# The last layer norm of a one-layer decoder step: statistics of two token tiles and the sample rows on ScalarE, the sample rows' normalising on ScalarE and GpSimd

## What is computed

```python
def layer_norm(x, g, b):
    xf = x.astype(F32)
    mu = jnp.mean(xf, -1, keepdims=True)
    var = jnp.mean(jnp.square(xf - mu), -1, keepdims=True)
    return ((xf - mu) * lax.rsqrt(var + LN_EPS) * g.astype(F32) + b.astype(F32)).astype(x.dtype)
...
xp = layer_norm(DN_ALPHA * xp + ff, ln2_g[l], ln2_b[l])
y_prompt = xp[:, N_META:]
...
xs = layer_norm(DN_ALPHA * xs + ff, ln2_g[l], ln2_b[l])
```

## Time and profile before

| | |
|---|---|
| time, median of three executions | 1506.05 us (1503.6, 1506.05, 1509.25) |
| span of the profiled execution, first to last instruction | 1499.4 us |
| TensorE busy | 1348.8 us, 90% |
| VectorE busy | 437.9 us, 29% |
| ScalarE busy | 327.1 us, 22% |
| GpSimd busy | 316.9 us, 21% |
| mean granted TensorE clock | 0.957 |
| VectorE's work in the last norm | 1474.05 to 1496.60 us |

### The profile page before, as it was taken

How to read it: one execution, slowest core, us unless ns; L and a number is a source line. 1 busy time by engine, 2 the same in 40 slices (tenths; PEclk the granted TensorE clock), 3 DMA queues, 4 the chain that set the end, 5 groups by cost and what they waited for, 6 DMA issues and landing times.

```text
span 1499.4 us, 32889 instructions
## 1 busy us (share of the span) xinstructions
PE 1348.8 (90%) x13060; PEld 663.9 (44%) x13060; DVE 437.9 (29%) x1016; ACT 327.1 (22%) x760; POOL 316.9 (21%) x328
## 2 busy tenths in 40 slices
PE   7999899889799999898999989899998988999980
PEld 6878677655423343232434323343433333333330
DVE  2311553757643221111221112122111311211225
ACT  1103001550003132122223212231321213222120
POOL 5214200112512122211112211111221111131012
PEclk9999998799779999999999999999999999999995
DMA  9355011350368999999999999999999999999953
GB/s 304 74 122 94 14 38 35 96 229 29 141 259 339 410 406 406 409 412 411 408 411 404 405 410 412 408 405 409 400 408 413 409 408 400 408 401 410 417 204 118
DMA packets 100515, 460.85 MB, mean 307 GB/s; under 512 B 30482, under 2 KB 40862, under 8 KB 51200
## 3 DMA queue, kind: packets, MB, share of 16 engines
q1 hardware_dynamic: 81440, 426.48, 70.5%
q0 software_dynamic: 18336, 30.14, 8.1%
q10 hardware_dynamic: 592, 2.13, 0.4%
HBM read 442.21 MB, written 22.37 MB: 310 GB/s over the span
## 4 chain that ended last, share of the span: by engine, by line
PE 42%; DMA 21%; DVE 8%; SPq 6%; issue 2%; ACT 0%; ACTq 0%; POOL 0%; DVEq 0%; POOLq 0%
PE PS L1379 19%; DMA ring<-in_w_moe_dram 19%; PE PS L1401 14%; PE PS L1281 4%; SPq L489 4%; DVE mix L1954 2%; PE PS L1392 1%; PE PS L1361 1%; DVE qmT L1961 1%; DVE qmT L1959 1%; SPq L497 1%; PE PS L1371 1%; DVE qmT L1955 1%; DVE qmT L1958 1%; DMA smalls<-token_lists 1%
## 5 line engine op out<-in xcount | busy, mean ns | idle before, releaser
L1379 PE MATMUL PS<-ring,mix 128*32 128x512 f32 x5376 | 605.8, 598 | 52.9 <-DMA ring<-in_w_moe_dram 41.9
L1379 PEld LDWEIGHTS PS<-ring,mix 128*32 128x32 f32 x5376 | 165.0, 110 | 453.4 <-issue 346.2
L769 POOL DMA_INDIRECT expert_rows<-mix,smalls x84 | 112.4, 1339 | 796.0 <-issue 510.6
L1954 DVE TENSOR_TENSOR mix<-PS,kn 128x512 f32<-128x512 f32 x84 | 58.1, 692 | 575.0 <-PE PS L1379 569.6
L965 ACT ACTIVATE mix<-PS,smalls 32x256 f32<-32x256 f32 x336 | 156.9, 467 | 177.4 <-PE PS L1401 174.3
L1401 PE MATMUL PS<-ring,mix 128*32 128x256 f32 x3328 | 187.0, 380 | 0.0
L1401 PEld LDWEIGHTS PS<-ring,mix 128*32 128x32 f32 x3328 | 104.7, 110 | 69.5 <-issue 0.5
L949 ACT COPY mix<-PS 128x512 f32<-128x512 f32 (+1 forms) x48 | 24.0, 535 | 466.3 <-PE PS L1371 466.3
L760 POOL DMA_INDIRECT mix<-x_rows,smalls x84 | 87.0, 1035 | 59.7 <-issue 53.1
L1051 PE MATMUL PS<-xT,ring 128*128 128x280 f32 x384 | 96.0, 412 | 0.0
L1039 PE MATMUL PS<-ring,xT 128*128 128x256 f32 (+1 forms) x480 | 86.9, 370 | 0.6 <-ACT mix L826 0.4
(11 more groups left out here) (376 smaller groups left out, 974.7 us busy)
## 6 DMA issues: line engine op xcount, KB each, us to landing
ring<-in_w_moe_dram SPq DMA_DIRECT2D x320, 1024.0 KB, 21.4
xT<-in_w_moe_dram SPq DMA_DIRECT2D x32, 1024.0 KB, 23.7
X<-in_w_moe_dram SPq DMA_DIRECT2D x32, 1024.0 KB, 27.0
ring<-in_w_in_dram SPq DMA_DIRECT2D x9, 1024.0 KB, 17.6
ring<-in_w_out_dram SPq DMA_DIRECT2D x4, 1024.0 KB, 5.0
X<-in_x_prompt_dram SPq DMA_DIRECT2D x4, 512.0 KB, 5.5
ring<-in_state_mlstm_C_dram POOLq DMA_DIRECT2D x1, 2048.0 KB, 16.2
ring<-in_w_in_dram SPq DMA_DIRECT2D x8, 256.0 KB, 10.5
```

What stands on the lines that cost most here:

```text
L769: nc.gpsimd.indirect_dma_start(out=y_dram, out_offset=bass.IndirectOffsetOnAxis(ap=lists[a][0:32, g, 1:2].bitcast(U32), axis=0), in_=ysb[g ...
L1379: ins = mm(bank(BANK0[a] + g)[32 * t:32 * t + 32, :], xgT[XBUF[a][g]][:, P * (k % 2) + 32 * (k // 2):P * (k % 2) + 32 * (k // 2) + 32], sl ...
L1954: link(V.tensor_tensor(ht, bank(BANK0[a] + g), b1b, ALU.add))
```

## The change

- SyncE loads the sample rows third instead of fifth, and stores them last, after the wait for `z_small` instead of the fifth `f_done`.
- VectorE makes `bn_stats` statistics of tiles 0 and 1 alone, both ahead of the first wide pass. It makes all eight wide passes of the prompt tiles; for tiles 2 and 3 they take negative mean and rstd from `zneg` and `zsq`, which come from the other engines. It does nothing for the sample rows.
- ScalarE sums the rows of the sample rows, tile 2 and tile 3 (`row_sums`, an Identity activation with an accumulated output, written to unused PSUM), and after GpSimd has made the negative mean it sums the squares of z - mean (`row_squares`). It also makes (z - mean) * rstd of the sample rows.
- GpSimd makes the means (`mean_of`), the powers of all five tiles (`counted_spread`, `spread_of`), the product -mean * rstd of the sample rows (`zbias`), and multiplies the sample rows by the gain and adds the bias, 8 x 1024 elements each. These are one fixed sequence.
- 16 columns of `smalls` and six semaphores are new. No other part of the program is edited.

```diff
--- before.py
+++ after.py
@@ -255,13 +255,13 @@
         cst = ctx.enter_context(nc.sbuf_tensor("cst", [P, 4, P], F32))
         ident, strict, causal, ones = (cst[:, i, :] for i in range(4))
         GC = ctx.enter_context(nc.sbuf_tensor("GC", [P, NT + 1, 68], F32))
-        sm_t = sb("smalls", 1280)
+        sm_t = sb("smalls", 1300)
         small_at = [0]
 
         def sml(n, rows=P):
             a = small_at[0]
             small_at[0] += n
-            assert small_at[0] <= 1280
+            assert small_at[0] <= 1300
             return sm_t[0:rows, a:a + n]
 
         def chunk(s):
@@ -389,6 +389,8 @@
         gsum = sml(5)
         tokid = sml(5)
         cadd, prime = sml(2), sml(4 * PRIME, 1)
+        zsum, zsq, zneg = sml(NT + 1), sml(NT + 1), sml(NT + 1)
+        zbias = sml(1, NS)
         lists = [sml(2 * n).bitcast(I32).rearrange("p (g c) -> p g c", c=2) for n in (4, 2, 4, 2)]
         raw = [sml(4 * n).rearrange("p (g w) -> p g w", w=4) for n in (4, 2, 4, 2)]
         def by_half(v, half):
@@ -440,6 +442,7 @@
         y_out = [sem(f"y_out{i}") for i in range(4)]
         gt_mm, gt_cp, b2_mm, y_ready = (sem(n) for n in ("gt_mm", "gt_cp", "b2_mm", "y_ready"))
         f_done, y_set, f_chain = (sem(n) for n in ("f_done", "y_set", "f_chain"))
+        z_sum, z_mean, z_sq, z_pow, z_unit, z_small = (sem(n) for n in ("z_sum", "z_mean", "z_sq", "z_pow", "z_unit", "z_small"))
         s_abc, s_scaled, gt_ready = sem("s_abc"), sem("s_scaled"), sem("gt_ready")
         steps = sem("steps")
         x_in = [sem(f"x_in{i}") for i in range(NT + 1)]
@@ -614,15 +617,14 @@
             for b in range(4, 6):
                 sp.wait_ge(xg_in[b], 16 * ROUNDS * XUSE[b])
             sp.wait_ge(shift_out, 32)
-            for tt in range(NT + 1):
+            for tt in (0, 1, NT, 2, 3):
                 r = NS if small(tt) else P
                 sp.dma_start(zb[tt][0:r, :], y_dram[P * tt:P * tt + r, :]).then_inc(x_in[tt], 16)
-            for tt in range(NT + 1):
+            for tt in range(NT):
                 sp.wait_ge(f_done, tt + 1)
-                if small(tt):
-                    sp.dma_start(y_sample.rearrange("b o d -> (b o) d"), zb[tt][0:NS, :]).then_inc(fin_out, 16)
-                else:
-                    sp.dma_start(y_prompt[0, P * tt:P * tt + P, :], zb[tt]).then_inc(fin_out, 16)
+                sp.dma_start(y_prompt[0, P * tt:P * tt + P, :], zb[tt]).then_inc(fin_out, 16)
+            sp.wait_ge(z_small, 1)
+            sp.dma_start(y_sample.rearrange("b o d -> (b o) d"), zb[NT][0:NS, :]).then_inc(fin_out, 16)
             sp.wait_ge(fin_out, 16 * (NT + 1))
 
 
@@ -794,14 +796,39 @@
                     for g in range(GROUPS[2]):
                         scatter(q * 4 + PER * ROUNDS, 2, g, [q * 16 + 16 * (ROUNDS * YUSE[b] + PRIME) for b in range(4)])
 
-            for tt in range(NT + 1):
+            def mean_of(n, tt):
                 r = NS if small(tt) else P
+                pool.wait_ge(z_sum, n + 1)
+                nc.gpsimd.tensor_scalar(zneg[0:r, tt:tt + 1], zsum[0:r, tt:tt + 1], -1.0 / D, None, ALU.mult).then_inc(z_mean, 1)
+
+            def spread_of(n, tt):
+                r = NS if small(tt) else P
+                o = zsq[0:r, tt:tt + 1]
+                pool.wait_ge(z_sq, n + 1)
+                link(nc.gpsimd.tensor_scalar(o, o, 1.0 / D, EPS, ALU.mult, ALU.add))
+                link(nc.gpsimd.tensor_tensor(o, o, powc[0:r, 0:1], ALU.pow), z_pow)
+                if small(tt):
+                    nc.gpsimd.tensor_tensor(zbias, zneg[0:r, tt:tt + 1], o, ALU.mult).then_inc(z_pow, 1)
+
+            def counted_spread(tt):
                 pool.wait_ge(ln_stat, NT + tt + 2)
-                if tt >= 2:
-                    pool.wait_ge(f_done, tt - 1)
-                o = rs2[0:r, tt % 2, 0:1]
-                link(nc.gpsimd.tensor_scalar(o, bag[0:r, 2 * (tt % 2) + 1:2 * (tt % 2) + 2], 1.0, EPS, ALU.mult, ALU.add))
-                nc.gpsimd.tensor_tensor(o, o, powc[0:r, 0:1], ALU.pow).then_inc(ln_pow, 1)
+                o = rs2[:, tt, 0:1]
+                link(nc.gpsimd.tensor_scalar(o, bag[:, 2 * tt + 1:2 * tt + 2], 1.0, EPS, ALU.mult, ALU.add))
+                nc.gpsimd.tensor_tensor(o, o, powc[:, 0:1], ALU.pow).then_inc(ln_pow, 1)
+
+            zs = zb[NT][0:NS, :]
+            mean_of(0, NT)
+            counted_spread(0)
+            mean_of(1, 2)
+            counted_spread(1)
+            spread_of(0, NT)
+            mean_of(2, 3)
+            spread_of(1, 2)
+            pool.wait_ge(ln_in, 64)
+            pool.wait_ge(z_unit, 1)
+            link(nc.gpsimd.tensor_tensor(zs, zs, lng[0:NS, :], ALU.mult))
+            spread_of(2, 3)
+            nc.gpsimd.tensor_tensor(zs, zs, lnb[0:NS, :], ALU.add).then_inc(z_small, 1)
 
 
         @block.scalar
@@ -1003,6 +1030,28 @@
                         if g:
                             weighted(group, 2, g - 1, q * 16 + 16 * (ROUNDS * YUSE[g - 1] + PRIME))
                     weighted(group, 2, 3, q * 16 + 16 * (ROUNDS * YUSE[3] + PRIME))
+
+            aside = PS[:, 0:2, :].rearrange("p b n -> p (b n)")
+
+            def row_sums(tt):
+                r = NS if small(tt) else P
+                act.wait_ge(x_in[tt], 48 if small(tt) else 32)
+                link(nc.scalar.activation(aside[0:r], zb[tt][0:r, :], ACT.Identity, accum_out=zsum[0:r, tt:tt + 1]), z_sum)
+
+            def row_squares(n, tt):
+                r = NS if small(tt) else P
+                act.wait_ge(z_mean, n + 1)
+                link(nc.scalar.activation(aside[0:r], zb[tt][0:r, :], ACT.Square, bias=zneg[0:r, tt:tt + 1],
+                                          accum_out=zsq[0:r, tt:tt + 1]), z_sq)
+
+            row_sums(NT)
+            row_sums(2)
+            row_squares(0, NT)
+            row_sums(3)
+            row_squares(1, 2)
+            act.wait_ge(z_pow, 2)
+            nc.scalar.activation(zb[NT][0:NS, :], zb[NT][0:NS, :], ACT.Identity, scale=zsq[0:NS, NT:NT + 1], bias=zbias).then_inc(z_unit, 1)
+            row_squares(2, 3)
 
 
         @block.tensor
@@ -1997,24 +2046,25 @@
             dve.wait_ge(ln_in, 64)
 
             def row_statistics(tt):
-                r = NS if small(tt) else P
-                dve.wait_ge(x_in[tt], 48 if small(tt) else 32)
-                if tt >= 2:
-                    dve.wait_ge(ln_pow, NT + tt)
+                dve.wait_ge(x_in[tt], 32)
                 for half in range(2):
-                    link(V.bn_stats(bst[0:r, 6 * half:6 * half + 6], zb[tt][0:r, 512 * half:512 * half + 512]))
-                link(V.bn_aggr(bag[0:r, 2 * (tt % 2):2 * (tt % 2) + 2], bst[0:r, :]), ln_stat)
-
-            row_statistics(0)
-            for tt in range(NT + 1):
-                r, z = NS if small(tt) else P, zb[tt]
-                z = z[0:r, :]
-                if tt < NT:
-                    row_statistics(tt + 1)
-                link(V.tensor_scalar(nbias[0:r], bag[0:r, 2 * (tt % 2):2 * (tt % 2) + 1], -1.0, None, ALU.mult))
-                link(V.scalar_tensor_tensor(z, z, nbias[0:r], lng[0:r, :], ALU.add, ALU.mult))
-                dve.wait_ge(ln_pow, NT + tt + 2)
-                link(V.scalar_tensor_tensor(z, z, rs2[0:r, tt % 2, 0:1], lnb[0:r, :], ALU.mult, ALU.add), f_done)
+                    link(V.bn_stats(bst[:, 6 * half:6 * half + 6], zb[tt][:, 512 * half:512 * half + 512]))
+                link(V.bn_aggr(bag[:, 2 * tt:2 * tt + 2], bst), ln_stat)
+
+            for tt in range(2):
+                row_statistics(tt)
+            for tt in range(NT):
+                z = zb[tt]
+                if tt < 2:
+                    link(V.tensor_scalar(nbias, bag[:, 2 * tt:2 * tt + 1], -1.0, None, ALU.mult))
+                else:
+                    dve.wait_ge(z_sq, tt)
+                link(V.scalar_tensor_tensor(z, z, nbias if tt < 2 else zneg[:, tt:tt + 1], lng, ALU.add, ALU.mult))
+                if tt < 2:
+                    dve.wait_ge(ln_pow, NT + tt + 2)
+                else:
+                    dve.wait_ge(z_pow, tt + 1)
+                link(V.scalar_tensor_tensor(z, z, rs2[:, tt, 0:1] if tt < 2 else zsq[:, tt:tt + 1], lnb, ALU.mult, ALU.add), f_done)
 
 
 def constants():
```

## The result

Over 20 executions of each, the changed kernel takes 1508.36 us (median) and the one before 1505.3: ratio 1.0022, 95% interval 1.0014 to 1.0031. It is slower by 3.1 us by the medians and 3.3 by the ratio (2.1 to 4.7 by its interval), where 0.6 less was forecast.

The account below looks back on a forecast made before the run. TensorE and weight transfers fill most of the chain; only VectorE's last norm moves: 1488.35 plus waits 0.5, 0.5, 1.9, 2.0, 0.8 = 1494.0, wide addition to 1496.0, store 2.8, span 1498.8 (-0.6), time 1505.4 us; range 1500 to 1509.

Parts of the forecast that it names:

- the norm: Last stretch, from VectorE's first statistic to the span's end, 25.4 us; the only part forecast to move, by -0.6.
- The sample store is issued at 1496.63 and the span ends at 1499.4, so 2.8 us lie behind VectorE.: Kernel's end before the change: 2.8 us from sample store to span end, reused behind GpSimd's wide addition to give 1498.8.
- The 3.85 us behind a last store of a prompt tile: End of kernel: if a 512 KB tile store is last, the span ends 2.14 + 1.67 after its issue, 3.85 after VectorE.
- The 1.67 taken over from the small store: End of kernel: time from the small store's last data to the span's end, assumed the same behind a tile's store.
- Ties at tiles 0 and 1: Last norm: GpSimd's power loses to VectorE's first pass, so the second pass waits 0.5 us at each tile.
- Tile 2: Last norm: VectorE's second pass waits 1.9 us for a power queued behind GpSimd's sample-row operations.
- The first wide operation: Tile 3 of the last norm: GpSimd's wide multiply of the sample rows holds VectorE's next pass 2.0 us.
- Spread of tile 3: Last norm: GpSimd's power for tile 3 runs after VectorE's first pass there, a wait of 0.8 us.
- A wide operation: GpSimd's multiply or addition of 1024 columns on 8 partitions: taken as 2.0 us, between 1.0 and 2.07.
- Rival (a): Slower: GpSimd's wide addition goes ahead of VectorE's last tile pass; +0.5 us, 1506.5, up to 1508; chance 0.25.
- (c): Slower: ScalarE leaves its overflow loop late, so tile 0 waits; about 3 us lost, 1508.5; chance 0.05.
- Rival (b): Faster: GpSimd wins the ties, tiles 0 and 1 wait nothing, tile 2 about 0.6; 1503.1, bound 1498.85; chance 0.25.

Follow-up runs that it names:

- f2_columns: Kernel before with the 16 new columns ahead of the lists, smalls 1300 wide, no new semaphores: ratio 1.0027 to the kernel before.
- g2_columns_1280: Kernel before with the 16 new columns ahead of the lists, smalls kept at 1280: ratio 1.0020 to the kernel before.
- h2_raw: Kernel before with only the raw rows (written by one small DMA per expert) moved within smalls: ratio 1.0011 to the kernel before.
- i2_raw_again: Kernel before with only the raw rows moved within smalls, measured a second time: ratio 1.0018 to the kernel before.
- f3_placed: Changed kernel with its columns in a tensor behind all others and its semaphores taken last: ratio 1.0005 to the kernel before, norm 26.24 us.
- e3_no_wide: Changed kernel without GpSimd's two wide operations (sample rows lack gain and bias): ratio 0.9986 to the kernel before, norm 21.93 us.
- e2_late_pool: Kernel before plus one unread one-column GpSimd operation after VectorE's last pass: ratio 1.0020 to the kernel before, norm 29.27 us.
- h4_one_power_again: Changed kernel with one joint power for tiles 2, 3 and sample rows, their wide passes on VectorE, columns ending smalls: ratio 0.9968 to the kernel before.
- e kernels: Four variants measured together on one chip: layout only, late GpSimd operation, no wide operations, sample passes on VectorE; ratios 1.0017, 1.0020, 0.9986, 0.9988 to before.
- g3_after_1280: Changed kernel with smalls at 1280 instead of 1300: ratio 1.0021 to the kernel before, norm 25.73 us.

## Why the prediction was wrong

- *Sum and sign.* Forecast -0.6 (1505.4), measured +3.1 by medians of 20 and +3.3 by the ratio; the norm alone +0.3 for -0.6. The larger part is a cost that the forecast put at nothing without a reason: 1.9 to 3.0 us in the expert stage by the raw rows' move (f2_columns, g2_columns_1280, h2_raw, i2_raw_again without any change of the norm, each against the traces of its own letter with the rows in place). "16 columns of smalls" stood in the change's description and got no price; what hides it was not asked. 0.3 and 1.9 to 3.0 make 2.2 to 3.3. The prediction had named this sign itself: it is wrong "if the weights' stage before 1466 changes its length".
- *"The sample store is issued at 1496.63 and the span ends at 1499.4, so 2.8 us lie behind VectorE."* This step failed. Of the 2.8, SyncE's part was 2.0 (1498.6), and the end was set by GpSimd's drain, 6.2 us behind its last operation. The rows of L237 would have shown it. So the sum should have followed GpSimd's end, not VectorE's: in the forecast's own times its wide addition ended at 1496.0, + 6.5 = 1502.5, 3.1 us more than the kernel before. That this is near the whole measured loss is chance: the norm lost 0.3, because GpSimd's last operation came 19.17 after VectorE's start and not 1496.0 - 1474.05 = 21.95. By e2_late_pool, each microsecond by which GpSimd's last operation ends later than in the kernel before (1492.9) costs one.
- *The 3.85 us behind a last store of a prompt tile* were 3.3 until SyncE was done (1500.00 to 1503.3), plus 0.2 to 0.3 when nothing else is late. The 1.67 taken over from the small store held some 0.5 in which only the drain was still running.
- *Ties at tiles 0 and 1* were forecast lost, 0.5 each; GpSimd won both in the profiled execution (0), and lost the first in f3_placed and e3_no_wide (0.55, the forecast's size). The mechanism was right, the outcome at tile 0, a race of 0.1 us, cannot be told from rows. The forecast of tile 1 failed in all four.
- *Tile 2*: 1.9 forecast, 1.27 measured, since the queue began earlier: the sample rows' power fell under the second pass of tile 1 and not the first of tile 2. *The first wide operation*: 2.0 and 1.95. *Spread of tile 3*: 0.8 and 1.16.
- *A wide operation* was put at 2.0; its own time is 2.19, above the upper bound of 2.07 too (which is not two of 1.005, 2.01). The figure of the Trainium skill (GPSIMD Engine Reference, Elementwise: side-by-side cycle accounting), by which 2.25 was estimated, was the better one.
- *Rival (a)* happened: the addition went ahead of VectorE's last pass and held it 1.62. Its price, 0.5, was worked out behind the wrong end; it had the right sign, and so had (c).
- *Rival (b)* was right for the two ties and nothing else. *(c)* happened only in small, and not by ScalarE's loop: GpSimd did wait for the sample rows' sum, 0.35 here and 0.79 in f3_placed, but ScalarE itself had been waiting for the rows to land. VectorE felt it only where the tie at tile 0 was lost by it. No table load stood before the sums.

## What to carry to other kernels

Before moving work to GpSimd near the end of a program, read when its last instruction ends and what its closing drain then takes: here the program never ended earlier than 6.4 us after it, whatever the other engines did. Wide operations of GpSimd beside two-input passes of VectorE were not parallel: each held the other, and few rows are not cheap (8 rows of 1024 took 2.19 us, 128 rows of 512 took 1.0); one-column powers can be joined in one instruction. New small buffers went behind the old ones without a cost that shows (f3_placed, h4_one_power_again), and a variant with only the new layout should be timed by itself.

## What the runs showed of the hardware that was not expected

- GpSimd's closing drain ended 6.2 to 6.4 us after its last operation, whether that was a one-column power, a wide addition or an unread scalar operation (e2_late_pool), and the span ended 6.42 to 6.63 us after the operation in every trace where the drain came last.
- The place of 192 bytes per partition, written by 32 small DMAs, changed a stage of 982.5 us by 1.9 to 3.0 us (0.9 to 1.7 on the chip of the e kernels), in good part at the experts whose list is in one of the four buffers, while all else stayed.
- A GpSimd operation that waits for VectorE's pass gets in between two passes that are 0.06 us apart (the multiply of 1491.65: its pass ended at 1492.66, and that of 1492.72 was held). A power that starts 0.08 or 0.09 ahead of a pass is not held (g3_after_1280; 1486.09, 0.57 us), and one that starts 0.06 behind it is (e3_no_wide, 1.67 us).
